# Tile addresses on multiples of 2,048 bytes, paired attention products and normalised probabilities in a two-layer trunk

## Chip, cores and metric

The kernel runs on one core of a Trainium2 chip. The metric is the device time of one execution in microseconds (us). TensorE multiplies a stationary tile, loaded by LDWEIGHTS, with a moving tile that streams past it, and writes PSUM; VectorE (DVE), ScalarE (ACT) and GpSimd (POOL) work on SBUF and PSUM; SyncE (SP) issues most DMAs. The engines run side by side and wait for each other by semaphores.

## What is computed

A trunk of two layers over x of 256 tokens and 1,024 channels, all float32. Cut to what matters:

```python
for l in range(2):
    x = x + 0.5 * swiglu(rms_norm(x, g1), w_gate, w_up, w_down)      # 1024 -> 2816 -> 1024
    z = rms_norm(x, gm) @ w_in[l]                                     # 1024 -> 4 * 512
    q, k, v, p = z split in four                                      # 8 heads of 64
    a = softmax(q @ k.T / 8 + bias, 256 keys, masked) @ v             # per head
    m = pool_scale * (group-linear of (mean over a window of p - p))  # 4 groups of 128
    x = x + concat([a, m]) @ w_out[l]
    x = x + 0.5 * swiglu(rms_norm(x, g2), w_gate2, w_up2, w_down2)
return rms_norm(x, final_norm)
```

## The kernel before, in words

Tokens lie in two tiles of 128 partitions (`t`). Each float32 product of weights is made from three float32r products: weights and activations are split into a high and a low part, and high x high, high x low and low x high are summed (`split_products`, L983, L984 and L986, inside `out_tile`, `down`, `gate_up` and `project_z`; `project_first` has its own copies at L993, L994 and L1043). Every one has a stationary tile of 128 x 128 and moves 512 columns. The weights come by DMA into three slots `w_raw`; ScalarE writes `w_hi` (L467, L474), VectorE writes `w_lo` (L714, L723). The stationary tiles are `xt_hi`/`xt_lo` (normalised activations, transposed; also the input of the output projection) and `gt_hi`/`gt_lo` (gated activations, transposed).

A layer is a feed-forward stage of eleven chunks, a mix stage, and a feed-forward stage. The order on each engine is the order in which its block is written; each engine works through its own list and waits where a semaphore is not there yet.

In the mix stage TensorE's list is `project_z` for the four parts of z (q, k, p, v; eight steps of three matmuls for each token tile), with other work put in behind given steps: transposes of q and k, scores of a head `s(h)` (`head_scores`, L1192, two products of 64 rows, each run as two passes of float32), and transposes of a head's probabilities `t(h)` (L1210). Then follow the pool differences (`pool_differences`, L1235), the pool's linear maps (L1244), probabilities x V (`probs_v`, L1220: the probabilities stationary, 64 columns of V moving), the output projection's first half, the transposes of the heads (L1308) and its second half.

Between them VectorE adds the bias and takes the row maximum (`add_bias`, L830 to L840), ScalarE takes the exponential with its row sum (`exps`, L615), TensorE transposes the unnormalised probabilities, and both engines store the transposed ones over `scores` (`store_probs_t`, L623 and L846). The division by the row sum comes last: one reciprocal for all heads (L900), and two products over the heads' output in PSUM (L915), which is then transposed and split (L669, L923).

SBUF tiles are taken one behind the other in the order of their `sb(...)` lines. Of the sizes in bytes per partition: each w tile 8,192, `resid` and `normed` 8,192, `xt_hi` and `xt_lo` 8,192, `gains` 192, each of three `gain_rows` 512, `final_gain` 4,096, `silu` and `gated` 2,048, `gt_hi` and `gt_lo` 4,096, `bias` 12,288, `mask` 256, `z` 16,384.

Of the kernel before, what the change touches and what calls it, by code (L numbers as in the profile page):

```python
# [24 lines left out]
D_MODEL = 1024  # L25
# [9 lines left out]
N_GROUPS = len(POOL_WINDOWS)  # L35
D_FF = 2816
RMS_EPS = 1e-6

P = 128
# [12 lines left out]
WARM_UP = 8  # L52

# [33 lines left out]
def trunk(nc, x, ffn1_norm, ffn1_w_gate, ffn1_w_up, ffn1_w_down, mix_norm, w_in, rpb, w_pool,  # L87
# [8 lines left out]
    with ctx:  # L96
# [9 lines left out]
        w_lo = [sb(f"w_lo{s}", [P, UNIT], F32R) for s in range(SLOTS)]  # L106
        resid = sb("resid", [P, TT, D_MODEL])
        normed = sb("normed", [P, TT, D_MODEL])
        xt_hi = sb("xt_hi", [P, TT, KT, P], F32R)
        xt_lo = sb("xt_lo", [P, TT, KT, P], F32R)  # L110
        gains = sb("gains", [P, STAGES, DEPTH, KT])
        gain_rows = [sb(f"gain_rows{j}", [DEPTH * KT, P]) for j in range(STAGES)]
        final_gain = sb("final_gain", [P, D_MODEL])
        silu = sb("silu", [P, TT, FC])
        gated = sb("gated", [P, TT, FC])
        gt_hi = sb("gt_hi", [P, 2, 2, TT, P], F32R)
        gt_lo = sb("gt_lo", [P, 2, 2, TT, P], F32R)
        bias = sb("bias", [P, N_HEADS, DELTAS, GRID_W])
        mask = sb("mask", [P, GRID_W])
# [3 lines left out]
        scores = sb("scores", [P, N_HEADS, TT, SEQ])  # L123
        pool_m = sb("pool_m", [P, TT, N_GROUPS, SEQ])
        w_pool_sb = sb("w_pool_sb", [P, N_GROUPS, P])
        pool_scale_sb = sb("pool_scale_sb", [P, N_GROUPS])
        ident = sb("ident", [P, P])
# [4 lines left out]
        zeros = sb("zeros", [P, BANK], F32R)  # L132
# [9 lines left out]
        row_sum = sb("row_sum", [P, TT, N_HEADS])  # L142
        inv_sum = sb("inv_sum", [P, TT, N_HEADS])
# [11 lines left out]

        def heads_out(t):
            return z[:, t, 0, :]
# [56 lines left out]
        heads_stored = sem("heads_stored")  # L214
        heads_t_ready = sem("heads_t_ready")
# [206 lines left out]
        def _(act):  # L422
# [188 lines left out]
            def exps(layer, h):  # L611

                act.wait_ge(max_ready, layer * N_HEADS + (h + 1))
                for t in range(TT):
                    done = nc.scalar.activation(  # L615
                        scores[:, h, t, :], scores[:, h, t, :], ACT.Exp,
                        bias=neg_max[:, h, t:t + 1], accum_out=row_sum[:, t, h:h + 1])
                done.then_inc(probs_ready, 1)
# [7 lines left out]
            def mix_stage(layer):  # L626
# [40 lines left out]
                for t in range(TT):  # L667
                    act.wait_ge(heads_t_ready, layer * 2 + (t + 1))
                    nc.scalar.activation(xt_hi[:, t, 0:4, :], ps[:, 6 + t, :], ACT.Copy  # L669
                                         ).then_inc(heads_t_hi_ready, 1)  # L670
# [31 lines left out]
        def _(dve):  # L702
# [145 lines left out]

            def store_diffs(layer, j):

                dve.wait_ge(diff_ready, layer * 2 + (j + 1))
                nc.vector.tensor_copy(z[:, j, 1, :], ps[:, 4 + j, :]).then_inc(diff_stored, 1)

            def mix_stage(layer):
# [38 lines left out]
                store_probs_t(layer, 5)  # L893
                store_diffs(layer, 0)
# [3 lines left out]

                dve.wait_ge(probs_ready, layer * N_HEADS + N_HEADS)
                nc.vector.reciprocal(inv_sum[:, :, :], row_sum[:, :, :]).then_inc(inv_ready, 1)  # L900
# [11 lines left out]
                dve.wait_ge(inv_ready, layer + 1)  # L912
                dve.wait_ge(pv_ready, layer * N_HEADS + N_HEADS)
                for t in range(TT):
                    nc.vector.tensor_tensor(  # L915
                        heads_out(t).rearrange("p (h d) -> p h d", h=N_HEADS),
                        ps[:, t, :].rearrange("p (h d) -> p h d", h=N_HEADS),
                        inv_sum[:, t, :].rearrange("p (h o) -> p h o", o=1)
                        .to_broadcast([P, N_HEADS, HEAD_DIM]), ALU.mult).then_inc(heads_stored, 1)
                mix_unit(layer, 10)  # L920
                for t in range(TT):
                    dve.wait_ge(heads_t_hi_ready, layer * 2 + (t + 1))
                    nc.vector.tensor_tensor(  # L923
                        xt_lo[:, t, 0:4, :], ps[:, 6 + t, :].rearrange("p (k q) -> p k q", k=4),
                        xt_hi[:, t, 0:4, :].bitcast(F32), ALU.subtract
                    ).then_inc(heads_t_lo_ready, 1)
# [52 lines left out]
        def _(pe):  # L979
# [206 lines left out]
            def head_scores(layer, h):  # L1186
                if h >= 2:

                    pe.wait_ge(biased_ready, layer * N_HEADS + (h - 1))
                rows = slice((h % 2) * HEAD_DIM, (h % 2 + 1) * HEAD_DIM)  # L1190
                for t in range(TT):
                    last = nc.tensor.matmul(ps[:, 4 + h % 2, t * SEQ:(t + 1) * SEQ],  # L1192
                                            q_t[rows, h // 2, t, :], k_t[rows, h // 2, :, :],
                                            start=True, stop=True)
                last.then_inc(scores_ready, 1)
# [19 lines left out]
            def probs_v(layer, h):  # L1215
                wait_probs_t_stored(layer, h)
                for t in range(TT):
                    for k in range(TT):

                        last = nc.tensor.matmul(  # L1220
                            ps[:, t, h * HEAD_DIM:(h + 1) * HEAD_DIM],
                            scores[:, h, k, t * P:(t + 1) * P],
                            z[:, k, 3, h * HEAD_DIM:(h + 1) * HEAD_DIM],
                            start=(k == 0), stop=(k == TT - 1))
                last.then_inc(pv_ready, 1)

            def pool_differences(layer, j):
# [5 lines left out]
                for g in (2 * j, 2 * j + 1):  # L1233
                    for k in range(TT):
                        last = nc.tensor.matmul(  # L1235
                            ps[:, 4 + j, (g % 2) * SEQ:(g % 2 + 1) * SEQ],
                            z[:, k, 2, g * P:(g + 1) * P], pool_m[:, k, g, :],
# [17 lines left out]
            def mix_stage(layer):  # L1255
# [19 lines left out]
                def s(h):  # L1275
                    if h == 0:
                        pe.wait_ge(k_t_stored, layer * 2 + 2)
                    head_scores(layer, h)

                def t(h):  # L1280
# [16 lines left out]
                for h in range(N_HEADS):  # L1297
                    probs_v(layer, h)

                pe.wait_ge(pooled_lo_ready, layer * N_GROUPS + N_GROUPS)  # L1300
                out_tile(layer, 0, 8, 0, True, start=True)
                for k in (1, 2, 3):
                    out_tile(layer, 0, 8 + k // 2, k % 2, True)

                for t in range(TT):
                    pe.wait_ge(heads_stored, layer * 2 + (t + 1))
                    for k in range(4):
                        last = nc.tensor.transpose(ps[:, 6 + t, k * P:(k + 1) * P],  # L1308
                                                   heads_out(t)[:, k * P:(k + 1) * P], ident[:, :])
                    last.then_inc(heads_t_ready, 1)  # L1310
                out_tile(layer, 1, 8, 0, False, start=True)
                out_tile(layer, 1, 8, 1, False).then_inc(w_out_used, 1)
                out_tile(layer, 1, 9, 0, False)
                out_tile(layer, 1, 9, 1, False).then_inc(w_out_used, 1)
                for t in range(TT):
                    pe.wait_ge(heads_t_lo_ready, layer * 2 + (t + 1))
                    for j in (10, 11):
                        for k in range(2):
# [72 lines left out]
```

## Time and profile before

| | us |
|---|---|
| median of 3 runs | 972.66 (971.89 to 972.71) |
| profiled execution | 971.49 |
| its span, first to last instruction | 969.5 |
| TensorE busy | 952.6 (98%) |
| VectorE busy | 548.3 (57%) |
| ScalarE busy | 496.9 (51%) |
| mean granted TensorE clock | 0.997 |

The page gives each engine's busy time, the span in 40 slices, and the costliest groups. Matmuls are pipelined: a row's duration contains the time in which the next one already runs, so the durations add up to more than the span. What a stream of matmuls costs is read from the starts of neighbouring rows. LDWEIGHTS stands under PEld.

### The profile page before, as it was taken

To read this page: it belongs to the slowest core of one execution; us is meant where nothing else is said; L and a number is where in the kernel's file an instruction comes from. 1 tells how busy PE (TensorE), PEld (TensorE's weight loads), DVE (VectorE), ACT (ScalarE), POOL (GpSimd) and SP (SyncE) were. 2 spreads that over 40 slices of the span, in tenths; PEclk is the share of its full clock that TensorE was granted. 3 is DMA by queue.
4 is the path that set the end of the run, shared out by engine and by line. 5 is a ranking of instruction groups with operands and counts; after the bars stand their busy time and mean duration, and the time that the engine had idled before them with its cause. 6 is when DMAs were issued, how large, how long until landed. Compare 5 with 4: busy or idle time off the path is not lost.

```text
span 969.5 us, 12851 instructions
## 1 busy us (share of the span) xinstructions
PE 952.6 (98%) x4379; PEld 777.3 (80%) x4379; DVE 548.3 (57%) x862; ACT 496.9 (51%) x813; POOL 44.7 (5%) x81
## 2 busy tenths in 40 slices
PE   8899999999999999999999999999999999999996
PEld 6688888877788888888888888888778888888885
DVE  5545564557645664655476555455755565455644
ACT  5545454556535554545465455455663365454542
POOL 1010010010001010100010000000100010000000
PEclk9999999999999999999999999999999999999999
DMA  7967868636224978675456657553542266556441
GB/s 242 248 189 175 234 171 281 233 104 242 88 87 136 255 175 227 175 212 186 130 181 214 215 195 250 180 191 124 173 174 88 87 217 212 178 180 209 152 151 44
DMA packets 123532, 174.67 MB, mean 180 GB/s; under 512 B 8384, under 2 KB 99696, under 8 KB 123248
## 3 DMA queue, kind: packets, MB, share of 16 engines
q1 hardware_dynamic: 117744, 165.70, 51.4%
q0 software_dynamic: 2848, 6.38, 5.5%
q10 hardware_dynamic: 2912, 2.22, 0.7%
q8 instruction: 18, 0.29, 0.1%
q14 instruction: 10, 0.08, 0.0%
HBM read 173.14 MB, written 4.19 MB: 183 GB/s over the span
## 4 chain that ended last, share of the span: by engine, by line
PE 93%; DVE 2%; ACT 2%; issue 2%; DMA 1%; SPq 0%; POOL 0%; POOLq 0%; DVEq 0%; ACTq 0%
PE ps L983 28%; PE ps L986 27%; PE ps L984 27%; PE ps L1080 2%; PE ps L1192 2%; PE ps L1220 1%; DVE w_lo L723 1%; PE ps L993 1%; PE ps L994 1%; PE ps L1210 1%; ACT xt_hi L489 1%; PE ps L1235 1%; PE ps L1068 1%; DMA w_raw<-in_ffn_w_down_dram 1%; DVE xt_lo L737 0%
## 5 line engine op out<-in xcount | busy, mean ns | idle before, releaser
L983 PE MATMUL ps<-w_hi,xt_hi 128*128 128x512 f32 x856 | 342.0, 400 | 3.0 <-DVE w_lo L723 1.5
L723 DVE SCALAR_TENSOR_TENSOR w_lo<-w_raw,gains,w_hi 128x512 fp32r<-128x512 f32 x416 | 285.1, 746 | 89.0 <-ACT w_hi L474 87.9
L984 PE MATMUL ps<-w_lo,xt_hi 128*128 128x512 f32 x856 | 333.5, 390 | 0.0
L986 PE MATMUL ps<-w_hi,xt_lo 128*128 128x512 f32 x856 | 329.2, 391 | 0.0
L474 ACT ACTIVATE w_hi<-w_raw,gains 128x512 fp32r<-128x512 f32 x408 | 260.7, 713 | 86.1 <-PE ps L986 81.1
L714 DVE TENSOR_TENSOR w_lo<-w_raw,w_hi 128x1024 fp32r<-128x1024 f32 x104 | 122.7, 1221 | 126.3 <-ACT w_hi L467 126.2
L983 PEld LDWEIGHTS ps<-w_hi,xt_hi 128*128 128x128 f32 x856 | 160.8, 188 | 41.4 <-DVE w_lo L723 4.1
L986 PEld LDWEIGHTS ps<-w_hi,xt_lo 128*128 128x128 f32 x856 | 160.7, 188 | 34.6
L984 PEld LDWEIGHTS ps<-w_lo,xt_hi 128*128 128x128 f32 x856 | 161.0, 188 | 30.3
L467 ACT ACTIVATE w_hi<-w_raw 128x1024 fp32r<-128x1024 f32 x104 | 104.4, 1051 | 114.0 <-PE ps L986 106.6
L983 PE MATMUL ps<-w_hi,gt_hi 128*128 128x512 f32 x352 | 139.0, 395 | 3.6 <-DVE gt_lo L778 3.6
L984 PE MATMUL ps<-w_lo,gt_hi 128*128 128x512 f32 x352 | 138.7, 394 | 0.0
L986 PE MATMUL ps<-w_hi,gt_lo 128*128 128x512 f32 x352 | 110.3, 393 | 0.0
L531 ACT ACTIVATE gt_hi<-ps 128x512 fp32r<-128x512 f32 x40 | 23.9, 597 | 139.8 <-PE ps L1080 139.8
L778 DVE TENSOR_TENSOR gt_lo<-ps,gt_hi 128x512 fp32r<-128x512 f32 x40 | 27.7, 691 | 105.4 <-ACT gt_hi L531 105.4
L983 PEld LDWEIGHTS ps<-w_hi,gt_hi 128*128 128x128 f32 x352 | 66.5, 189 | 18.6 <-DVE gt_lo L778 4.0
L984 PEld LDWEIGHTS ps<-w_lo,gt_hi 128*128 128x128 f32 x352 | 66.6, 189 | 14.1
L986 PEld LDWEIGHTS ps<-w_hi,gt_lo 128*128 128x128 f32 x352 | 66.4, 189 | 14.2
L772 DVE SCALAR_TENSOR_TENSOR gated<-ps,rstd_scaled,silu 128x256 f32<-128x256 f32 x88 | 42.0, 477 | 11.1 <-ACT silu L542 11.1
L542 ACT ACTIVATE silu<-ps,rstd 128x256 f32<-128x256 f32 x88 | 41.5, 472 | 8.8 <-PE ps L986 4.2
L387 POOL DMA_DIRECT2D bias_scratch<-in_rpb_dram x32 | 26.4, 828 | 217.9 <-PE ps L986 209.9
L737 DVE TENSOR_TENSOR xt_lo<-ps,xt_hi 128x512 fp32r<-128x512 f32 x24 | 15.5, 686 | 21.4 <-ACT xt_hi L489 21.4
(87 smaller groups left out, 434.7 us busy)
## 6 DMA issues: line engine op xcount, KB each, us to landing
w_raw<-in_ffn_w_down_dram SPq DMA_DIRECT2D x88, 512.0 KB, 4.3
w_raw<-in_ffn_w_gate_dram SPq DMA_DIRECT2D x86, 512.0 KB, 4.1
w_raw<-in_ffn_w_up_dram SPq DMA_DIRECT2D x86, 512.0 KB, 5.2
w_raw<-in_w_in_dram SPq DMA_DIRECT2D x32, 512.0 KB, 4.9
w_raw<-in_w_out_dram SPq DMA_DIRECT2D x16, 512.0 KB, 5.2
bias_scratch<-in_rpb_dram POOLq DMA_DIRECT2D x32, 96.0 KB, 7.9
bias<-bias_scratch POOLq DMA_DIRECT2D x2, 1536.0 KB, 7.1
pool_m<-in_pool_matrix_dram ACTq DMA_DIRECT2D x1, 1024.0 KB, 8.3
```

What stands on the lines that cost most here:

```text
L387: pool.dma_start(scratch[number, rq * GRID_W:(rq + 1) * GRID_W, i, :] .rearrange("p (d c) -> d p c", d=DELTAS), src).then_inc(bias_rows_lo ...
L467: nc.scalar.activation(w_hi[slot][:, part], w_raw[slot][:, part], ACT.Copy).then_inc(hi_ready[slot], 2)
L474: nc.scalar.activation(w_hi[slot][:, part], w_raw[slot][:, part], ACT.Copy, scale=g).then_inc(hi_ready[slot], 1)
L531: nc.scalar.activation(gt_hi[:, 0, :, :, :], ps[:, 6, :], ACT.Copy).then_inc(gt_hi_ready, 1)
L542: nc.scalar.activation(silu[:, t, :], ps[:, t, 0:FC], ACT.Silu, scale=rstd[:, t, :]).then_inc(silu_ready[t], 1)
L714: nc.vector.tensor_tensor(w_lo[slot][:, part], w_raw[slot][:, part], w_hi[slot][:, part].bitcast(F32), ALU.subtract).then_inc(lo_ready[slo ...
L723: nc.vector.scalar_tensor_tensor(w_lo[slot][:, part], w_raw[slot][:, part], g, w_hi[slot][:, part].bitcast(F32), ALU.mult, ALU.subtract).t ...
L772: nc.vector.scalar_tensor_tensor(gated[:, t, :], ps[:, t, FC:2 * FC], rstd_scaled[:, t, 0:1], silu[:, t, :], ALU.mult, ALU.mult).then_inc( ...
L778: nc.vector.tensor_tensor(gt_lo[:, 0, :, :, :].rearrange("p k t q -> p (k t q)"), ps[:, 6, :], gt_hi[:, 0, :, :, :].rearrange("p k t q -> ...
L983: nc.tensor.matmul(o, hi, wh, start=start, stop=False)
L984: nc.tensor.matmul(o, hi, wl, start=False, stop=False)
L986: last = nc.tensor.matmul(o, lo, wh, start=False, stop=bool(stop))
```

## The change

A pad of 480 words stands in front of all tiles, and the list of tiles is put in another order: first w, xt, gt and zeros, then silu, gated, resid, normed, z, q_t, k_t, scores and the rest whose sizes are multiples of 2,048 bytes, and the small ones last. The scores of two heads are made together (`pair_scores`), the products on rows 0 to 63 and on rows 64 to 127 in turn. Probabilities are normalised on VectorE before they are transposed (`normalise`). V is stationary in `pair_v`, with 64 columns for each head of a pair in its own half of the columns, and moves 256 columns of transposed probabilities; its output is already transposed, so the transposes of the heads and the products with inv_sum go. The second half of the tokens in the pool differences moves only the columns from 120. The order of the mix stage on TensorE and VectorE is written anew.

```diff
+POOL_FROM = 128 - max(POOL_WINDOWS) // 2
+PAGE_PAD = 480
+        sb("page_pad", [P, PAGE_PAD])
         w_raw = ...; w_hi = ...; w_lo = ...
+        xt_hi, xt_lo, gt_hi, gt_lo, zeros, silu, gated
         resid, normed
-        xt_hi, xt_lo, gains, gain_rows, final_gain, silu, gated, gt_hi, gt_lo, bias, mask
         z, q_t, k_t, scores
+        bias, pool_m, final_gain, w_pool_sb, ident, gain_rows, mask, gains
...
+            def normalise(layer, h):
+                dve.wait_ge(probs_ready, layer * N_HEADS + (h + 1))
+                nc.vector.reciprocal(inv_sum[:, h, :], row_sum[:, h, :]).then_inc(inv_ready, 1)
+                dve.wait_ge(inv_ready, layer * N_HEADS + (h + 1))
+                for t in range(TT):
+                    done = nc.vector.tensor_scalar(scores[:, h, t, :], scores[:, h, t, :],
+                                                   inv_sum[:, h, t:t + 1], None, ALU.mult)
+                done.then_inc(normalised_ready, 1)
...
 (VectorE, mix_stage)
                 add_bias(layer, 0)
                 add_bias(layer, 1)
                 mix_unit(layer, 7, halves=(0,))
+                normalise(layer, 0)
+                normalise(layer, 1)
                 add_bias(layer, 2)
+                add_bias(layer, 3)
                 mix_unit(layer, 7, halves=(1,))
-                add_bias(layer, 3)
+                normalise(layer, 2)
+                store_probs_t(layer, 1)
                 add_bias(layer, 4)
-                store_probs_t(layer, 1)
+                normalise(layer, 3)
                 add_bias(layer, 5)
                 mix_unit(layer, 8)
+                normalise(layer, 4)
+                store_probs_t(layer, 3)
+                normalise(layer, 5)
                 add_bias(layer, 6)
-                store_probs_t(layer, 3)
                 add_bias(layer, 7)
                 store_kv(layer, 3, 0)
+                normalise(layer, 6)
                 store_probs_t(layer, 5)
+                normalise(layer, 7)
...
-                for t in range(TT):
-                    nc.vector.tensor_tensor(heads_out(t) ..., ps[:, t, :] ..., inv_sum ..., ALU.mult)
...
+            def pair_scores(layer, pair):
+                if pair >= 1:
+                    pe.wait_ge(biased_ready, layer * N_HEADS + 2 * pair)
+                for t in range(TT):
+                    for e in range(2):
+                        rows = slice(e * HEAD_DIM, (e + 1) * HEAD_DIM)
+                        last = nc.tensor.matmul(ps[:, 4 + e, t * SEQ:(t + 1) * SEQ],
+                                                q_t[rows, pair, t, :], k_t[rows, pair, :, :],
+                                                start=True, stop=True)
+                        if t == TT - 1:
+                            last.then_inc(scores_ready, 1)
...
 (transpose_probs)
-                pe.wait_ge(probs_ready, layer * N_HEADS + (h + 1))
+                pe.wait_ge(normalised_ready, layer * N_HEADS + (h + 1))
...
+            def pair_v(layer, pair):
+                wait_probs_t_stored(layer, 2 * pair)
+                wait_probs_t_stored(layer, 2 * pair + 1)
+                cols = slice((pair % 2) * SEQ, (pair % 2 + 1) * SEQ)
+                for k in range(TT):
+                    for e in range(2):
+                        h = 2 * pair + e
                         last = nc.tensor.matmul(
-                            ps[:, t, h * HEAD_DIM:(h + 1) * HEAD_DIM],
-                            scores[:, h, k, t * P:(t + 1) * P],
+                            ps[e * HEAD_DIM:(e + 1) * HEAD_DIM, pair // 2, cols],
                             z[:, k, 3, h * HEAD_DIM:(h + 1) * HEAD_DIM],
+                            scores[:, h, k, :],
                             start=(k == 0), stop=(k == TT - 1))
...
-                project_z(layer, 2, 1, after={1: lambda: s(1), 3: lambda: s(2),
-                                              5: lambda: (s(3), t(0)), 7: lambda: (s(4), t(1))})
-                project_z(layer, 3, 0, after={1: lambda: (s(5), t(2)), 3: lambda: (s(6), t(3)),
-                                              5: lambda: (s(7), t(4)), 7: lambda: t(5)})
+                project_z(layer, 2, 1, after={3: lambda: s(1), 5: lambda: t(0),
+                                              7: lambda: (s(2), t(1))})
+                project_z(layer, 3, 0, after={1: lambda: t(2), 3: lambda: (s(3), t(3)),
+                                              5: lambda: t(4), 7: lambda: t(5)})
```

## Rows read from the trace of the kernel before

**Rows 1.** The page: busy time of each engine, and the granted clock in 40 slices.
```profile
PE 952.6 (98%) x4379; PEld 777.3 (80%) x4379; DVE 548.3 (57%) x862; ACT 496.9 (51%) x813; POOL 44.7 (5%) x81
PEclk9999999999999999999999999999999999999999
```

**Rows 2.** TensorE's waits: who waited for whom; us in total, times, longest.
```profile
PE ps L983 <- DVE gt_lo L778: 3.6, 1, 3.6
PE ps L983 <- DVE w_lo L723: 1.5, 3, 1.1
PE ps L993 <- ACT xt_hi L489: 1.2, 5, 0.2
```

**Rows 3.** Timeline, gate and up products: start us, duration us, instruction.
```profile
62.06 0.39 PE L983 MATMUL ps<-w_hi,xt_hi 128*128 128x512 f32 x1
...
65.46 0.39 PE L983 MATMUL ps<-w_hi,xt_hi 128*128 128x512 f32 x1
```

**Rows 4.** Timeline, first down product, and what follows the last.
```profile
73.40 0.39 PE L983 MATMUL ps<-w_hi,gt_hi 128*128 128x512 f32 x1
...
78.90 0.39 PE L983 MATMUL ps<-w_hi,xt_hi 128*128 128x512 f32 x1
```

**Rows 5.** Timeline, two products of the output projection.
```profile
289.21 0.39 PE L983 MATMUL ps<-w_hi,xt_hi 128*128 128x512 f32 x1
...
291.93 0.39 PE L983 MATMUL ps<-w_hi,xt_hi 128*128 128x512 f32 x1
```

**Rows 6.** Timeline behind the longest wait, with the halved clock.
```profile
38.64 0.63 PE L984 MATMUL ps<-w_lo,gt_hi 128*128 128x512 f32 x1
39.07 0.63 PE L983 MATMUL ps<-w_hi,gt_hi 128*128 128x512 f32 x1
39.50 0.63 PE L984 MATMUL ps<-w_lo,gt_hi 128*128 128x512 f32 x1
```

**Rows 7.** Chain of work, mix stage of layer 0: start us, us, what.
```profile
261.99 1.73 PE ps L1235 x8
...
270.40 7.09 PE ps L1220 x64
...
283.04 0.87 PE ps L1308 x8
```

**Rows 8.** Windows: all engines; L983 alone; L993 alone (us, busy, PEclk, DMA).
```profile
38.60:39.50 0.90, 0.90 (x4) 0.67 (x3) 0.90 (x2) 0.90 (x3) 0.00 (x0) 0.50 1.15 135
...
40.00:969.50 929.50, 466.47 (x1174) 1.00 0.57 178
...
40.00:969.50 929.50, 16.18 (x40) 1.00 0.57 178
```

**Rows 9.** Timeline around one head's scores.
```profile
234.82 0.40 PE L986 MATMUL ps<-w_hi,xt_lo 128*128 128x512 f32 x1
235.15 1.13 PE L1192 MATMUL ps<-k_t,q_t 64*128 64x256 f32 x4
236.20 0.50 PE L983 MATMUL ps<-w_hi,xt_hi 128*128 128x512 f32 x1
236.54 0.39 PE L984 MATMUL ps<-w_lo,xt_hi 128*128 128x512 f32 x1
```

**Rows 10.** VectorE's groups: instruction, count, busy us, mean ns, idle before.
```profile
L974 DVE TENSOR_SCALAR normed<-z,rstd 128x512 f32<-128x512 f32 x1 | 0.5, 488 | 0.7 <-POOL rstd L417 0.7
L900 DVE RECIPROCAL inv_sum<-row_sum 128x16 f32<-128x16 f32 x2 | 0.5, 242 | 0.0
```

**Rows 11.** Timeline of VectorE and ScalarE around mix unit 8.
```profile
247.30 0.42 DVE L833 CUSTOM_DVE_ANT_0 scores<-ps,bias 128x256 f32<-128x256 f32 x1 [1.05 <-issue]
248.11 0.17 DVE L840 TENSOR_SCALAR neg_max<-row_max 128x2 f32<-128x2 f32 x1
248.18 0.68 DVE L846 COPY scores<-ps 128x512 f32<-128x512 f32 x1
251.40 0.50 ACT L615 ACTIVATE scores<-scores,neg_max 128x256 f32<-128x256 f32 x1
252.39 2.00 ACT L467 ACTIVATE w_hi<-w_raw 128x1024 fp32r<-128x1024 f32 x2
253.53 2.36 DVE L714 TENSOR_TENSOR w_lo<-w_raw,w_hi 128x1024 fp32r<-128x1024 f32 x2 [2.23 <-ACT w_hi L467]
```

More of the change, by code:

```diff
@@ L106, in trunk @@
         w_lo = [sb(f"w_lo{s}", [P, UNIT], F32R) for s in range(SLOTS)]
+        xt_hi = sb("xt_hi", [P, TT, KT, P], F32R)
+        xt_lo = sb("xt_lo", [P, TT, KT, P], F32R)
+        gt_hi = sb("gt_hi", [P, 2, 2, TT, P], F32R)
+        gt_lo = sb("gt_lo", [P, 2, 2, TT, P], F32R)
+        zeros = sb("zeros", [P, BANK], F32R)
+        silu = sb("silu", [P, TT, FC])
+        gated = sb("gated", [P, TT, FC])
         resid = sb("resid", [P, TT, D_MODEL])
         normed = sb("normed", [P, TT, D_MODEL])
[L109 to L119, printed above, removed]
         z = sb("z", [P, TT, 4, 512])
@@ L123, in trunk @@
         scores = sb("scores", [P, N_HEADS, TT, SEQ])
+        bias = sb("bias", [P, N_HEADS, DELTAS, GRID_W])
         pool_m = sb("pool_m", [P, TT, N_GROUPS, SEQ])
+        final_gain = sb("final_gain", [P, D_MODEL])
         w_pool_sb = sb("w_pool_sb", [P, N_GROUPS, P])
+        ident = sb("ident", [P, P])
+        gain_rows = [sb(f"gain_rows{j}", [DEPTH * KT, P]) for j in range(STAGES)]
+        mask = sb("mask", [P, GRID_W])
+        gains = sb("gains", [P, STAGES, DEPTH, KT])
         pool_scale_sb = sb("pool_scale_sb", [P, N_GROUPS])
-        ident = sb("ident", [P, P])
         wait_mark = sb("wait_mark", [P, 1])
@@ L666, in mix_stage @@
                 mix_unit(layer, 10)
-                for t in range(TT):
-                    act.wait_ge(heads_t_ready, layer * 2 + (t + 1))
-                    nc.scalar.activation(xt_hi[:, t, 0:4, :], ps[:, 6 + t, :], ACT.Copy
-                                         ).then_inc(heads_t_hi_ready, 1)
+                for b in range(2):
+                    act.wait_ge(pv_ready, layer * 4 + (2 * b + 2))
+                    nc.scalar.activation(
+                        xt_hi[:, :, 2 * b:2 * b + 2, :],
+                        ps[:, b, :].rearrange("p (g t q) -> p t g q", g=2, t=TT), ACT.Copy
+                    ).then_inc(heads_t_hi_ready, 1)
                 mix_unit(layer, 11)
@@ L897, in mix_stage @@
                 store_probs_t(layer, 7)
-                dve.wait_ge(probs_ready, layer * N_HEADS + N_HEADS)
-                nc.vector.reciprocal(inv_sum[:, :, :], row_sum[:, :, :]).then_inc(inv_ready, 1)
                 store_kv(layer, 3, 1)
@@ L911, in mix_stage @@
                         ALU.mult, ALU.subtract).then_inc(pooled_lo_ready, 1)
-                dve.wait_ge(inv_ready, layer + 1)
-                dve.wait_ge(pv_ready, layer * N_HEADS + N_HEADS)
-                for t in range(TT):
+                mix_unit(layer, 10)
+                for b in range(2):
+                    dve.wait_ge(heads_t_hi_ready, layer * 2 + (b + 1))
                     nc.vector.tensor_tensor(
[L916 to L925, printed above, removed]
+                        xt_lo[:, :, 2 * b:2 * b + 2, :],
+                        ps[:, b, :].rearrange("p (g t q) -> p t g q", g=2, t=TT),
+                        xt_hi[:, :, 2 * b:2 * b + 2, :].bitcast(F32), ALU.subtract
                     ).then_inc(heads_t_lo_ready, 1)
@@ L1184, in transpose_heads @@
                 last.then_inc(qk_t_ready, 1)
[L1186 to L1190, printed above, removed]
+            def pair_scores(layer, pair):
+                if pair >= 1:
+                    pe.wait_ge(biased_ready, layer * N_HEADS + 2 * pair)
                 for t in range(TT):
[L1192 to L1195, printed above, removed]
+                    for e in range(2):
[5 more added lines that the diff above has]
+                            last.then_inc(scores_ready, 1)
             def wait_probs_t_stored(layer, h):
@@ L1234, in pool_differences @@
                     for k in range(TT):
+                        first = POOL_FROM * k
                         last = nc.tensor.matmul(
-                            ps[:, 4 + j, (g % 2) * SEQ:(g % 2 + 1) * SEQ],
-                            z[:, k, 2, g * P:(g + 1) * P], pool_m[:, k, g, :],
+                            ps[:, 4 + j, (g % 2) * SEQ + first:(g % 2 + 1) * SEQ],
+                            z[:, k, 2, g * P:(g + 1) * P], pool_m[:, k, g, first:],
                             start=(k == 0), stop=(k == TT - 1))
@@ L1273, in heads_k, with s @@
                     transpose_heads(layer, 1, h)
-                def s(h):
-                    if h == 0:
+                def s(pair):
+                    if pair == 0:
                         pe.wait_ge(k_t_stored, layer * 2 + 2)
-                    head_scores(layer, h)
+                    pair_scores(layer, pair)
                 def t(h):
@@ L1296, in mix_stage @@
                 pe.wait_ge(z_kv_stored, layer * 4 + 4)
-                for h in range(N_HEADS):
-                    probs_v(layer, h)
+                for pair in range(N_HEADS // 2):
+                    pair_v(layer, pair)
                 pe.wait_ge(pooled_lo_ready, layer * N_GROUPS + N_GROUPS)
-                out_tile(layer, 0, 8, 0, True, start=True)
-                for k in (1, 2, 3):
-                    out_tile(layer, 0, 8 + k // 2, k % 2, True)
                 for t in range(TT):
[L1306 to L1314, printed above, removed]
+                    out_tile(layer, t, 8, 0, t == 0, start=True)
+                    last = out_tile(layer, t, 8, 1, t == 0)
+                    if t == 1:
+                        last.then_inc(w_out_used, 1)
+                    out_tile(layer, t, 9, 0, t == 0)
+                    last = out_tile(layer, t, 9, 1, t == 0)
+                    if t == 1:
+                        last.then_inc(w_out_used, 1)
                 for t in range(TT):
-                    pe.wait_ge(heads_t_lo_ready, layer * 2 + (t + 1))
                     for j in (10, 11):
+                        if t == 0:
+                            pe.wait_ge(heads_t_lo_ready, layer * 2 + (j - 9))
                         for k in range(2):
```

16 lines of the change are left out of this document (4 added, 12 removed).

## The prediction

> **What bounds the kernel now.** I read the page first: TensorE is busy 98% of the span, and its granted clock is full in all 40 slices [rows 1]. The waits of TensorE come next: the longest is 3.6 us, once, near the start, and all the others together are about 5 us [rows 2]. So nothing but TensorE's own stream sets the time from 40 us on, and what a matmul costs is the distance between the starts of two neighbours, not its duration. That distance is the third view, the timeline of single instructions. In the gate and up products 15 matmuls lie between 62.06 and 65.46 us: 226.7 ns each [rows 3]. In the down products 24 lie between 73.40 and 78.90 us: 229.2 ns each [rows 4]. In the output projection 12 lie between 289.21 and 291.93 us: 226.7 ns again [rows 5]. All have 512 columns of float32r, and there are 3,744 of them (856, 352 and 40 times three forms).
>
> The same instruction at the halved clock starts every 0.43 us [rows 6], with 0.50 as its clock [rows 8], and 512 columns at 1.2 GHz are 427 ns. Two array clocks per column of a float32 pass with 256 columns are also 512 clocks, and eight such passes take 1.73 us, 216 ns each [rows 7]. At full clock 512 clocks are 213.3 ns. So the float32r matmul, which reads its 2,048 bytes per partition at full rate, pays 11 to 13 ns that neither the half-rate pass nor the slow clock shows. The rest of the argument turns on what these 11 to 13 ns are.
>
> **Part 1: the addresses.** The pad of 480 words is 1,920 bytes, and if it brings the first tile to a multiple of 2,048, the tiles began at byte 128. By the sizes in the list, each 512-column slice of w_hi and w_lo then starts at 128 beyond such a multiple and crosses one boundary; xt_hi and xt_lo start at 128, and gt_hi and gt_lo, behind gains and gain_rows, at 1,856. After the change all start at 0 and no slice of w crosses. Two things bear on whether this matters. The output projection and the down products run the same helper with the same kind of w slices and the same order of PSUM banks. They differ in the stationary tile, xt against gt, and their pitches differ by 2.5 ns [rows 4, 5]. So an address, by all the rows show, does reach the pitch. And the slices of pool_m, at 64 beyond a multiple, cross a boundary in every second group, and all passes take 216 ns [rows 7]; a crossing that costs is thus one that the full read rate exposes, as is anything else that costs at full rate. The rows don't tell a crossing from a fixed cost of each float32r matmul. I take the crossing, because the pitch moved with an address in the one place where the rows allow a comparison.
>
> The pitch after is bounded by 213.3 and 226.7 ns (no change), and below a gain by the worse phase, 229.2 ns everywhere. I take 215.5, the float32 pass, which has the same count of array clocks. After 40 us there are 1,174 + 40 matmuls of each form [rows 8], some 3,640, of which 1,056 read gt. The sum is 2,584 x 11.2 ns = 28.9 us and 1,056 x 13.7 ns = 14.5 us: 43.4 us. What lies before 40 us is left out, since the first weights are still arriving: TensorE waits there for gt_lo [rows 2], whatever its pitch.
>
> Against this stands the Trainium skill, TensorE: Matmul & The Clock Gate, part 2, on loading the stationary operand: the engine has two independent SBUF read ports, and loading the next weights takes nothing from the running matmul. By that reading an address pair has no say, the 2.5 ns between xt and gt would be unexplained, and part 1 would bring nothing; it is rival A. The same page gives 215.7 ns for 512 columns of bf16 at full clock, which as an estimate would make the sum 42.6 us.
>
> **Part 2: score pairs in row halves.** Today each head is a visit of four passes with 64 rows. From the last projection matmul before to the second behind, 234.82 to 236.54 us, it takes 1.72 us [rows 9]; without a change of the array's shape this would be two distances of 0.227 and four of 0.216, 1.32 us. A visit thus costs 0.40 us of emptying and bare weight loads. Eight visits become four: 1.6 us per layer. Within a pair, two passes on one row half now alternate with two on the other. No row shows two halves at once. Bounds: nothing overlaps (0), or at each of the three changes of half one pass hides (3 x 0.216 x 4 pairs = 2.6 us). I take 2.6, since the halves share neither rows nor a PSUM bank.
>
> **Part 3: V stationary in column halves.** Today 64 passes with 64 columns take 7.09 us [rows 7], 111 ns each, the pace of the weight loads, as the transposes' 109 ns is. Then 32 passes of 256 columns come: serial 32 x 0.216 + 0.40 for a new shape = 7.3 us; with the halves side by side 17 x 0.216 + 0.40 = 4.1 us. The gain is between -0.2 and 3.0 us; I take 3.0, for the same reason as above. The Trainium skill's TensorEngine Tiling, key properties, says both things, that a change of mode drains the engine and that tiles run in parallel; the first agrees with the 0.40 us, the second no run here shows yet.
>
> **Part 4: small ones.** The head transposes go: 0.87 us per layer [rows 7]. The pool differences of the second token half shrink from 256 to 136 columns: 8 passes x (216 - 115) = 0.8 us. Fewer VectorE operations stand behind the heads, but nobody waited for them: four output tiles (5.4 us) lay between. The copy to xt_hi and xt_lo now has eight tiles (11 us) of cover for about 3 us of work. Without that cover it would cost those 3 us. The reordered tiles of other engines cost nothing that any row prices. No DMA and no queue order on SyncE or GpSimd is touched.
>
> **Part 5: what is added, normalise.** On VectorE, per head, a reciprocal (under 0.24 us) and two products of 256 columns. The nearest row is an SBUF to SBUF product of 512 columns at 0.49 us [rows 10]; I take 0.7 us per head until TensorE may go, bounds 0.5 and 1.0. Eight are 5.6 us per layer, on an engine busy 57% [rows 1]; the load is no matter, the order is. Transposes of head h now wait for normalise(h), and behind that wait the whole projection stream is queued. The worst place is t(4): normalise(4) stands behind mix_unit(8), which waits for ScalarE. From the end of the third score pair the chain is: transposes of head 1 and the signal 0.9, copy 0.6, add_bias(4) 0.9, normalise(3) 0.55, add_bias(5) 1.0, the exponentials 1.0, ScalarE's first half of unit 8 1.0, VectorE's two halves 2.3, normalise(4) 0.7 [rows 10, 11]: 9.0 us. TensorE has before t(4) three sets of four transposes (1.6), six steps of three matmuls (4.0) and a score pair (1.4): 7.0 us. It waits 2.0 us. By the same bookkeeping t(0) waits 0.4 us behind unit 7, the third pair 0.2 for its banks, t(6) 0.5: about 3.1 us per layer, and 0.4 more when the projection steps are shorter. Bounds: 1 and 5 us.
>
> **Sum.** Parts 2 to 4 give 1.6 + 2.6 + 3.0 + 0.9 + 0.8 = 8.9 us per layer, less 3.5 us of waits: 5.4, for two layers 10.8 us. With part 1: 54.2 us. The profiled execution took 971.5 us, with a span of 969.5; it would become 917.3. The median stands 1.2 us above it, so 918.5.
>
> **Rivals.** A: the 11 ns belong to every float32r matmul and stay. For it: there is no warm row of the same matmul at another w address. Against it: 226.7 against 229.2. Waits are then 3.1: 972.7 - 2 x 5.8 = 961; if only gt's 2.5 ns go (1,056 x 2.5 = 2.6 us), 958.5.
> B: the pitch falls, but the halves don't run side by side. Scores lose 2.6 and PV 3.2 us per layer, while t(4)'s wait shrinks by some 0.6: 918.5 + 2 x 5.2 = 929.
> C: part of the pitch goes (half): about 940.
> D: neither pays: 961 + 10.4 = 971.5, within 0.2%.
> E, slower: with every tile on a multiple of 2,048 stationary and moving reads always start in the same phase and collide. Its place is each float32r matmul, its price 3.7 us per ns of pitch. With the mix stage's gain of 11.6 it turns the sign from +3.1 ns; at +4 ns the time is 976. For it speaks only that the pitch does move with an address; against it, that xt and w start in the same phase today and are the faster pair.
>
> **How the numbers follow.** Forecast 0.42, A 0.33, B 0.12, C 0.06, D 0.04, E 0.03. The forecast's own range is 911 (pitch 213.4) to 927. For 8 in 10 the range must hold A as well, so it runs from 912 to 964; D, E and the ends of others are left out. A measurement of this kernel tells 0.2%, 2 us, from no change. Faster: all but D, E and a sliver, 0.93; same 0.04; slower 0.03.
>
> **What would show it.** The distance of two gate and up matmuls: 215.5 (forecast) or 226.7 (A). The down products should have the same distance, since their tile gets the same phase. A score pair of eight passes: 1.3 us side by side or 1.9 in a row. PV: 3.7 or 6.9 us. In the waits of TensorE new lines should stand, for VectorE's scores, some 6 us, the longest near 2 us at t(4). A pitch of 216 with a time above 935 would mean that another engine or the weights' DMA has become the bound in the feed-forward stages; busy shares of VectorE and ScalarE under 65% say no.

## The result, and the profile after

| | before | changed |
|---|---|---|
| median, us | 972.31 (971.89 to 972.71) | 960.17 (958.90 to 960.97) |
| ratio | | 0.9874, 95% interval 0.9857 to 0.9891 |
| profiled execution, us | 971.49 | 958.90 |
| its span, us | 969.5 | 957.0 |

The change makes the kernel 1.3% faster, 12.1 us. The forecast was 918.5 us, and the range from 912 to 964 held the time only because it reached to rival A, which had 961 or, with the 2.5 ns of gt, 958.5.

The page of the changed kernel, TensorE's busy time and the granted clock in 40 slices, as in [rows 1]:

```profile
PE 932.1 (97%) x4299; PEld 760.1 (79%) x4299; DVE 555.6 (58%) x904; ACT 496.2 (52%) x813; POOL 44.6 (5%) x81
PEclk9999999999999999999999999999999999999999
```

The timeline of the changed kernel gives the distances (start us, duration us, instruction). Between the first two rows lie 21 gate and up matmuls, between the third and the fourth 24 down products:

```profile
61.68 0.39 PE L992 MATMUL ps<-w_hi,xt_hi 128*128 128x512 f32 x1
...
66.44 0.39 PE L992 MATMUL ps<-w_hi,xt_hi 128*128 128x512 f32 x1
...
73.03 0.39 PE L992 MATMUL ps<-w_hi,gt_hi 128*128 128x512 f32 x1
...
78.47 0.39 PE L992 MATMUL ps<-w_hi,xt_hi 128*128 128x512 f32 x1
```

The gate and up products kept their 226.7 ns (4.76 us / 21), against [rows 3]. The down products went from 229.2 ns in [rows 4] to 226.7 (5.44 / 24). So by the sizes of the tiles no slice of w crosses a boundary any more, and the 11 ns are still there; only the 2.5 ns between xt and gt have gone. (No row shows an address: that the pad brings the first tile to a multiple of 2,048 bytes is taken from its size.)

The start of each stage shows where the 12.5 us of span came from. These are the first transposes of the residual in the mix stage, the second feed-forward stage, and the next layer's first; before, then changed:

```profile
202.85 0.82 PE L1068 MATMUL ps<-ident,resid 128*128 128x128 f32 x6
300.10 0.60 PE L1068 MATMUL ps<-ident,resid 128*128 128x128 f32 x4
488.27 0.93 PE L1068 MATMUL ps<-ident,resid 128*128 128x128 f32 x7
```

```profile
202.07 0.60 PE L1077 MATMUL ps<-ident,resid 128*128 128x128 f32 x4
294.08 0.92 PE L1077 MATMUL ps<-ident,resid 128*128 128x128 f32 x7
481.74 1.03 PE L1077 MATMUL ps<-ident,resid 128*128 128x128 f32 x8
```

The mix stage fell from 97.25 to 92.01 us, the feed-forward stage behind it from 188.17 to 187.66. In layer 1 the mix stage is 4.9 us shorter. Two mix stages make 10.1 us, the four feed-forward stages 2.0 and the start before the first 0.4.

In the mix stage a pair's scores now take what one head's took (1.72 us in [rows 9]): 1.74 us, from the last matmul before to the second behind. V's 32 passes end after 3.6 us, where 64 took 7.09 [rows 7]:

```profile
233.96 0.40 PE L995 MATMUL ps<-w_hi,xt_lo 128*128 128x512 f32 x1
234.29 1.13 PE L1202 MATMUL ps<-k_t,q_t 64*128 64x256 f32 x8
235.35 0.50 PE L992 MATMUL ps<-w_hi,xt_hi 128*128 128x512 f32 x1
235.70 0.40 PE L993 MATMUL ps<-w_lo,xt_hi 128*128 128x512 f32 x1
...
268.54 3.67 PE L1234 MATMUL ps<-scores,z 128*64 128x256 f32 x32
272.14 0.50 PE L992 MATMUL ps<-w_hi,xt_hi 128*128 128x512 f32 x1
```

Eight passes need four distances, 32 need sixteen: two always start together, 6 or 7 ns apart. And the waits of TensorE, which had no such lines in [rows 2] (us in total, times, longest):

```profile
PE ps L1221 <- DVE scores L856: 7.0, 6, 2.4
PE ps L992 <- DVE gt_lo L779: 3.6, 1, 3.6
...
PE ps L1202 <- DVE row_max L834: 1.0, 4, 0.3
```

The longest is the one of head 4:

```profile
254.49 0.66 PE L1221 MATMUL ps<-ident,scores 128*128 128x128 f32 x4 [2.36 <-DVE scores L856]
```

### The profile page after: what moved, and what is told of

Same layout as the page of the kernel before. It is cut to its first block and busy times, and to the rows that moved or that the text cites. A ratio compares the mean times of both kernels' runs of the same rounds, so it can differ in the third digit from the quotient of the medians.

```text
span 957.0 us, 12739 instructions
## 1 busy us (share of the span) xinstructions
PE 932.1 (97%) x4299; PEld 760.1 (79%) x4299; DVE 555.6 (58%) x904; ACT 496.2 (52%) x813; POOL 44.6 (5%) x81
## 5 line engine op out<-in xcount | busy, mean ns | idle before, releaser
L993 PE MATMUL ps<-w_lo,xt_hi 128*128 128x512 f32 x856 | 334.2, 390 | 0.0
L993 PEld LDWEIGHTS ps<-w_lo,xt_hi 128*128 128x128 f32 x856 | 161.4, 189 | 30.8
L993 PE MATMUL ps<-w_lo,gt_hi 128*128 128x512 f32 x352 | 137.7, 391 | 0.0
L993 PEld LDWEIGHTS ps<-w_lo,gt_hi 128*128 128x128 f32 x352 | 66.4, 189 | 13.6
```

The lines of the kernel that those rows point to most:

```text
L993: nc.tensor.matmul(o, hi, wl, start=False, stop=False)
```

## The experiments

Three questions: whether the addresses alone make the 2.5 ns, and by what rule; what the 11 ns are; and what stands behind the new waits.

### Addresses alone, and all the rest alone

The kernel before with the new list of tiles and the pad, nothing else:

```diff
+        sb("page_pad", [P, PAGE_PAD])
         w_raw, w_hi, w_lo
+        xt_hi, xt_lo, gt_hi, gt_lo, zeros, silu, gated, resid, normed, ...
```

> The kernel before with nothing but the pad and the new order of the tiles (part 1 alone). Theory S (the pitch follows the phase of the stationary tile against the moving one, and only gt was out of phase): the distance of the down products falls from 229.2 to 226.7 ns, that of gate and up products stays at 226.7; 1,056 x 2.5 ns = 2.6 us, so 969.7. Theory N (the addresses do nothing alone, and gt's pitch fell for another reason of the change): 972.3. The theory of the prediction (crossings cost 11 ns) would want 929.

Measured: 969.98 us, ratio 0.9971 (0.9960 to 0.9982) to the kernel before, 972.91 beside it: 2.9 us. The down products stand 226.9 ns apart in the mean, where 229.1 stood; those with xt do not change.

The changed kernel with the old list:

```diff
-        sb("page_pad", [P, PAGE_PAD])
+        (the list of the kernel before)
```

> The changed kernel with the old list of tiles and no pad (parts 2 to 5 alone). Theory S: down products at 229.2 ns again, 960.2 + 2.6 = 962.8. Theory N: 960.2, and the down products at 226.7. The mix stages should stay as in the changed kernel, 92.0 and 92.4 us.

Measured: 962.86 us, ratio 0.9904 (0.9892 to 0.9917). The distance of the down products is back; between these rows lie 24:

```profile
74.32 0.39 PE L991 MATMUL ps<-w_hi,gt_hi 128*128 128x512 f32 x1
...
79.81 0.39 PE L991 MATMUL ps<-w_hi,xt_hi 128*128 128x512 f32 x1
```

5.49 / 24 = 228.8 ns. Both came out within 0.3 us of theory S. The two parts add up: 2.9 us for the addresses and 10.0 for the rest, against 12.1 for the whole, of which each is known to about 1 us.

### What the 11 ns are

Rows of float32r matmuls on two tiles of ones, in place of the warm-up. The kernel ran once; what is read from it is the distances inside a row. A part of them:

```diff
-            for n in range(WARM_UP):
-                last = nc.tensor.matmul(ps[:, n % 2, :], zeros[:, 0:P], zeros[:, :], ...)
+            for n in range(13):
+                last = nc.tensor.matmul(ps[0:128, n % 2, 0:512], st[:, 0:128], mv[:, 256:768], ...)
+            for n in range(13):
+                last = nc.tensor.matmul(ps[0:128, n % 2, 0:256], st[:, 0:128], mv[:, 0:256], ...)
+            for n in range(13):
+                last = nc.tensor.matmul(ps[0:64, n % 2, 0:512], st[:, 0:64], mv[:, 0:512], ...)
```

> The changed kernel with rows of 13 float32r matmuls in place of the warm-up, all with the same two tiles of ones: moving and stationary start moved by 64, 128 and 1,024 bytes, 256 and 384 in place of 512 columns, 64 and 32 stationary columns, and a bf16 row. Its time is no measure of the change (some 40 us more). Theory F (11 to 13 ns are a fixed cost of each float32r matmul): 512, 384 and 256 columns cost 226.7, 173.3 and 120 ns, fewer stationary columns change nothing, bf16 216. Theory L (the weight load takes read slots from the moving stream): with 64 and 32 stationary columns the distance falls by half and three quarters of 13 ns, to 220 and 217. Theory C (a boundary crossed, the prediction's): moving starts moved by 64 and 128 bytes cost 11 ns more than the aligned ones. Theory S: a start moved by 64 bytes on one side alone gives 229.2, moved by 128 or on both sides 226.7.

The timeline of the probe, a row for each 13 matmuls: the moving start moved by 1,024 bytes (so that 512 columns cross a boundary), the stationary start moved by 64 bytes, then, further down, 256 columns, 384 columns, 64 and 32 stationary columns, and bf16:

```profile
23.36 3.16 PE L1356 MATMUL ps<-xt_hi,xt_lo 128*128 128x512 f32 x13
26.35 3.19 PE L1358 MATMUL ps<-xt_hi,xt_lo 128*128 128x512 f32 x13
...
38.40 1.72 PE L1366 MATMUL ps<-xt_hi,xt_lo 128*128 128x256 f32 x13
39.95 2.42 PE L1368 MATMUL ps<-xt_hi,xt_lo 128*128 128x384 f32 x13
42.20 3.15 PE L1370 MATMUL ps<-xt_hi,xt_lo 128*64 128x512 f32 x13
45.19 3.17 PE L1372 MATMUL ps<-xt_hi,xt_lo 128*32 128x512 f32 x13
48.20 2.98 PE L1374 MATMUL ps<-xt_hi,xt_lo 128*128 128x512 bf16 x13
```

After most changes of operands up to nine distances of a row with 512 columns are unsettled (224 to 238 ns), so a row's mean can be 4 ns above its settled value. Settled, from the last distances of a row, are: with the crossing 226.7, as without; 384 columns 173.3; 256 columns 120; bf16 216. Taken from these, 512, 384 and 256 columns at 2.4 GHz are 213.3, 160.0 and 106.7 ns, and each time 13.3 are left. So the rest is fixed for each float32r matmul and has nothing to do with the columns read: theory F. Theory C falls, since a crossed boundary costs nothing. Theory L falls too: with 64 and 32 stationary columns the distance does not shrink, it even grows, to 230 and 231.5; why is open. That the bf16 row has 2.6 ns in place of 13.3 says that this is a property of float32r, not of 512 columns. Why float32r has it is open.

Of the Trainium skill, TensorE: Matmul & The Clock Gate, part 1: N / 2.4 + 2.5 ns from start to start, for a matmul with N moving columns on the warm array. It holds for the bf16 row (216, it gives 215.7), not for float32r, where the last term is 13.3. The float32 passes of 256 columns stand 215.4 ns apart, which fits it only if each of their columns counts as two.

### The rule of the phase

Four rows of the first probe already differed with the starts, and not as theory S had it there. It wanted 229.2 ns for 64 bytes on either side and 226.7 for 128. The stationary start moved by 64 bytes gave 233.3, the moving one 228.9, and 128 bytes on either side 232.4; only 64 bytes on both sides came out as expected, 226.7. A second probe, also run once, moved the starts against each other:

> The changed kernel with rows of 20 float32r matmuls in place of the warm-up, stationary and moving starts moved against each other by 32 to 512 bytes. If the distance follows the difference of the two starts modulo 128 bytes, moves by 256 and 512 bytes cost nothing and those by 192 and 384 cost as 64 and 0. If modulo 256: 256 and 512 cost nothing, 192 on the stationary side costs what 64 on the moving side costs (229). If modulo 512: 256 costs something too.

Rows of 20, from its timeline. The stationary start was moved by 192, 256, 384, 512 and 64 bytes, in this order, then (next but one) the moving one by 192:

```profile
17.62 4.74 PE L1352 MATMUL ps<-xt_hi,xt_lo 128*128 128x512 f32 x20
22.20 4.72 PE L1354 MATMUL ps<-xt_hi,xt_lo 128*128 128x512 f32 x20
26.76 4.81 PE L1356 MATMUL ps<-xt_hi,xt_lo 128*128 128x512 f32 x20
31.41 4.70 PE L1358 MATMUL ps<-xt_hi,xt_lo 128*128 128x512 f32 x20
35.94 4.83 PE L1360 MATMUL ps<-xt_hi,xt_lo 128*128 128x512 f32 x20
...
45.27 4.83 PE L1364 MATMUL ps<-xt_hi,xt_lo 128*128 128x512 f32 x20
```

| stationary minus moving start, bytes | settled distance, ns |
|---|---|
| 0, 256, 512, -256, -512 | 226.7 |
| 192, -64 | 228.9 |
| 128, -128, 384 | 232.4 |
| -384 | 233.3 |
| 32, 64, -192 | 233.3 |

The difference counts modulo 256 bytes: 192 and -64 agree, 64 and -192 agree, 256 and 512 are as good as 0. Only -384 is 1 ns off the others of its class, which is open. In the kernel before gt starts at 1,856 and w at 128; 1,728 modulo 256 is 192, and its 229.2 ns are within 0.3 of the second line of the table. Even the single distances agree: both there and in the probe's row they go 226, 229, 232, 225, 230, 231. xt had a difference of 0. That is all that the addresses of part 1 were worth.

To see the rule in the kernel, 16 words between w and the rest:

```diff
+        sb("phase_pad", [P, 16])
         xt_hi = sb("xt_hi", [P, TT, KT, P], F32R)
```

> The changed kernel with 16 words between the w tiles and all tiles behind them, so that xt and gt start 64 bytes behind a multiple of 2,048 and w on one. Theory S with the distances of the probe (stationary start moved by 64 bytes: 233.5 ns, against 226.7): all float32r matmuls with both stationary tiles cost 6.8 ns more; some 3,640 of them after the start make 25 us: 985. The rival: in a kernel whose moving tile changes with each matmul the phase counts less than in the probe, the 2.5 ns of gt everywhere: 9 us, 969.

Measured, in two executions: 980.13 us, ratio 1.0086 (1.0066 to 1.0106) to 971.83 beside it: 20 us over the changed kernel, slower than the kernel before. The distance is the probe's; 21 matmuls lie between these rows, 4.90 / 21 = 233.3 ns:

```profile
62.81 0.39 PE L993 MATMUL ps<-w_hi,xt_hi 128*128 128x512 f32 x1
...
67.71 0.40 PE L993 MATMUL ps<-w_hi,xt_hi 128*128 128x512 f32 x1
```

The sum of 25 us was 5 too high. Part of that is that the distances behind transposes were never at 226.7 (in each chunk some six, of 228 to 236 ns), so they lose less; a feed-forward stage became 4.6 us longer (192.2, from 300.53 to 492.76 us, against 187.7), where 792 x 6.7 ns is 5.3.

And the changed kernel without its pad, so that all tiles start 128 bytes behind a multiple of 2,048:

```diff
-        sb("page_pad", [P, PAGE_PAD])
```

> The changed kernel without the pad, its list of tiles as it is: every tile that TensorE reads starts 128 bytes behind a multiple of 2,048, stationary and moving alike, and each 512-column slice crosses a boundary. Theory S (only the difference of the two starts modulo 256 bytes counts): nothing changes, 226.7 ns for all products and 960. The rival (the multiples of 2,048 are worth something by themselves): a distance over 227 ns, each ns of it 3.7 us.

Measured: 959.87 us, ratio 0.9888 (0.9869 to 0.9908). The distances are those of the changed kernel, 226.9 ns for the down products in the mean. The pad does nothing, and neither do the multiples of 2,048. A last probe, run once:

> The changed kernel with rows of 20 float32r matmuls in place of the warm-up. Both starts moved by 16, 32 and 128 bytes: if the difference alone counts, 226.7 for all; the probe before gave 228 to 232 for 16 bytes, so a start must also be a multiple of some 32 or 64 bytes. Then 64-row halves in turn: two float32r matmuls of 512 columns on the two row halves. If the fixed 13 ns belong to one stream of matmuls, the pair takes 226.7 ns together; if the two halves cover each other's 13 ns, 214 to 216. Last a row that stays in one PSUM bank: 226.7 if the bank has no say.

```profile
17.81 4.76 PE L1352 MATMUL ps<-xt_hi,xt_lo 128*128 128x512 f32 x20
22.41 4.74 PE L1354 MATMUL ps<-xt_hi,xt_lo 128*128 128x512 f32 x20
...
36.20 4.85 PE L1361 MATMUL ps<-xt_hi,xt_lo 64*128 64x512 f32 x40
40.98 4.85 PE L1363 MATMUL ps<-xt_hi,xt_lo 128*128 128x512 f32 x20
```

Both starts at 16 bytes gave 230 ns (first row, 229 and 231 in turn), both at 32 or 128 bytes 226.7. So an equal difference is not enough: 16 bytes behind a tile's start is a bad place for both, 32 bytes are a good one, and others than 16, 32, 64 and 128 were not run. The 40 matmuls on row halves start two by two, 3 to 4 ns apart, and a pair takes 226.7 once settled: the halves run side by side, but they don't cover each other's 13 ns. One PSUM bank instead of two makes no difference.

### The waits for normalised scores

First only the longest one:

```diff
                 add_bias(layer, 5)
-                mix_unit(layer, 8)
                 normalise(layer, 4)
                 store_probs_t(layer, 3)
+                mix_unit(layer, 8)
                 normalise(layer, 5)
```

> The changed kernel with normalise(4) and store_probs_t(3) ahead of mix_unit(8) in VectorE's list. If the longest wait (2.4 us in each layer, transposes of head 4) comes from VectorE standing at unit 8 while the exponentials of head 4 are long done, it goes, and 2 x 2.0 to 2.4 us come back: 955.4 to 956.2. The rival: what is late next is unit 8's low part or add_bias(6), which move back with it or stay where they were, and less than 1 us is won in all: over 959.

Measured: 957.04 us, ratio 0.9840 (0.9827 to 0.9853), between the two theories: 3.1 us won, not 4 to 5. The waits for normalised scores fell from 7.0 to 4.4 us, the longest from 2.4 to 1.1. Head 4 no longer waits; late next are heads 5 and 6, whose steps still stand behind unit 8.

```profile
PE ps L1221 <- DVE scores L856: 4.4, 6, 1.1
```

```profile
257.77 0.66 PE L1221 MATMUL ps<-ident,scores 128*128 128x128 f32 x4 [0.56 <-DVE scores L856]
260.94 0.66 PE L1221 MATMUL ps<-ident,scores 128*128 128x128 f32 x4 [1.12 <-DVE scores L856]
```

Then all of VectorE's list by when its input comes:

```diff
                 add_bias(layer, 1)
+                normalise(layer, 0)
+                normalise(layer, 1)
                 mix_unit(layer, 7, halves=(0,))
-                normalise(layer, 0)
-                normalise(layer, 1)
...
                 add_bias(layer, 5)
-                mix_unit(layer, 8)
                 normalise(layer, 4)
-                store_probs_t(layer, 3)
                 normalise(layer, 5)
                 add_bias(layer, 6)
+                store_probs_t(layer, 3)
                 add_bias(layer, 7)
-                store_kv(layer, 3, 0)
                 normalise(layer, 6)
+                mix_unit(layer, 8)
+                store_kv(layer, 3, 0)
```

> The changed kernel with VectorE's list in the order in which the scores and exponentials come: normalise(0) and (1) ahead of unit 7, normalise(4), (5), add_bias(6), (7) and normalise(6) ahead of unit 8. If the waits of TensorE for normalised scores and free banks (7.0 + 1.0 us) are all due to the place of the weight units, they go: 960.2 - 8 = 952.2, or 4.8 under the kernel with normalise(4) moved alone. The rival: the exponentials of ScalarE, queued behind its part of unit 8, are late next and leave 2 us or more of the waits: 954 or above.

Measured: 949.65 us, ratio 0.9776 (0.9763 to 0.9790), 10.5 us under the changed kernel, where 8 were expected, and the fastest of all. (The two were measured beside different runs of the kernel before; by the ratios it is 9.5 us.) None of the waits of the mix stage is left:

```profile
PE ps L992 <- DVE gt_lo L779: 3.3, 1, 3.3
PE ps L1343 <- DVE zeros L704: 1.5, 1, 1.5
PE ps L1002 <- ACT xt_hi L488: 1.2, 5, 0.2
```

Its mix stage runs from 202.18 to 289.42 us:

```profile
202.18 1.03 PE L1077 MATMUL ps<-ident,resid 128*128 128x128 f32 x8
289.42 0.82 PE L1077 MATMUL ps<-ident,resid 128*128 128x128 f32 x6
```

87.2 us against 92.0: 4.8 us for 4.0 us of listed waits. In layer 1 it is 87.2 against 92.4, 5.1 us, but there a wait for w_lo, 0.5 us in its row, is gone too. A wait costs more than its row. At t(4) of the changed kernel the last matmul before and the first transpose are 2.76 us apart, where the reordered kernel has 0.23, so the place costs 2.53 for the 2.36 of the row; and the four transposes then take 0.41 us in place of 0.35:

```profile
251.73 0.40 PE L995 MATMUL ps<-w_hi,xt_lo 128*128 128x512 f32 x1
254.49 0.66 PE L1221 MATMUL ps<-ident,scores 128*128 128x128 f32 x4 [2.36 <-DVE scores L856]
254.90 0.47 PE L992 MATMUL ps<-w_hi,xt_hi 128*128 128x512 f32 x1
```

### Halves not in turn

```diff
-                for t in range(TT):
-                    for e in range(2):
+                for e in range(2):
+                    for t in range(TT):
                         rows = slice(e * HEAD_DIM, (e + 1) * HEAD_DIM)
```

and the same in `pair_v`.

> The changed kernel with the same products, but both of one half before both of the other half, in the scores and in the products with V. In the changed kernel the passes start two by two, 7 ns apart, every 216 ns: 4 distances for a pair's scores, 16 for the products with V. Theory T (only neighbours in the list run side by side): a pair's eight passes take 7 distances (one overlap where the half changes), V's 32 passes 24 or 25; per layer 4 x 3 + 8 or 9 distances more, 4.4 us, for two layers up to 8.8 us, less what the waits for normalised scores take up: 965 to 969. The rival (the engine looks further ahead and pairs them anyway): 960.

Measured: 959.00 us, ratio 0.9870 (0.9855 to 0.9885): theory T falls. The eight passes of a pair still take no longer than in turn:

```profile
234.32 0.40 PE L995 MATMUL ps<-w_hi,xt_lo 128*128 128x512 f32 x1
234.65 1.14 PE L1202 MATMUL ps<-k_t,q_t 64*128 64x256 f32 x8
235.72 0.50 PE L992 MATMUL ps<-w_hi,xt_hi 128*128 128x512 f32 x1
236.05 0.39 PE L993 MATMUL ps<-w_lo,xt_hi 128*128 128x512 f32 x1
```

1.73 us, with two passes starting 13 ns apart in place of 7. With V the two are 13 and then 57 to 59 ns apart, and still there is one such pair every 216 ns. So the two halves need not alternate in the list: here four passes of one half stand before four of the other. The trace does not name the halves of a pair, and what looks ahead, and how far, these runs don't show.

## Why the prediction was wrong

**What bounds the kernel** was read rightly: TensorE's stream, and in it the distance between starts.

**Part 1 failed**, and in one sentence: "I take the crossing, because the pitch moved with an address in the one place where the rows allow a comparison." The two facts were separate. The 2.5 ns between xt and gt do come from an address, from the difference of two starts modulo 256 bytes, and they went as theory S says (2.9 us measured, 2.6 by the sum). The 11 to 13 ns are a fixed 13.3 ns of each float32r matmul, which rows at another width would have shown, and the trace of before has none. So 40.5 of the 43.4 us never existed. An effect of 2.5 ns was used as evidence for one of 11, and the sentence before it in the prediction had said that the rows can't tell the two apart; the chance of 0.42 against 0.33 did not follow from rows, and the likeliest case should have been the one in which only the 2.5 ns that the rows show go: 958.5, which is 1.7 from the median.

The sentence of the Trainium skill, TensorE: Matmul & The Clock Gate, part 2, on two independent read ports agrees with the probe as far as the 11 ns go: with 32 stationary columns in place of 128 the moving stream gains nothing. But the phase between the two starts costs up to 6.7 ns, so an address pair does have a say, which that sentence does not lead one to expect; where the two reads meet is open.

**Parts 2 and 3** were right in kind and too low. For the scores the prediction let three of eight passes hide, and four do; for V it had 15 of 32 hidden and 0.40 us for the new shape, where 16 are and the whole takes 3.60 us. Scores: 4 x 1.74 in place of 8 x 1.72 us, less the two matmuls' share of 0.454 in each visit: 10.1 to 5.1, a gain of 5.0 (4.2 forecast). V: 7.09 to 3.60, a gain of 3.5 (3.0). For V the outcome was partly luck: the reason given was that the halves share neither rows nor a PSUM bank, but the two column halves of `pair_v` use all rows and write the same bank.

**Part 4** was right: the sum of all gains, read from the reordered kernel that has no waits, is 97.25 - 87.24 = 10.0 us per layer, of which scores and V make 8.5, which leaves 1.5 for the transposes and the pool differences (1.7 forecast). The pool differences by themselves gave the 0.8 forecast: two rows of eight passes take 1.49 us each, where they took 1.89.

**Part 5** was right in place and mechanism. The waits came at t(4), t(0), t(6) and the third pair, 2.4, 0.5, 0.6 and 0.3 us in layer 0, where 2.0, 0.4, 0.5 and 0.2 stood (and 0.4 more in all with shorter steps); the fourth pair also waited 0.2 us, which the prediction did not have. In sum the list has 4.0 us per layer, and their cost is 4.8, where 3.1 to 3.5 was forecast. Normalise itself took 0.72 us for a head from its reciprocal to the next operation on VectorE, as taken.

So the mix stages gave 10.1 us where 10.8 were forecast, and that nearness is luck in part: per layer the errors in gross gain (+1.1) and in waits (+1.3) nearly cancel. **Rivals:** A held, with gt's 2.5 ns gone. B and D fell with the halves side by side, C with gate and up products that kept their 226.7 ns. E fell, and its mechanism is the wrong way round: it let equal starts collide, but equal starts are the ones that cost nothing, and unequal ones cost. Its price, 3.7 us per ns, was somewhat high: 64 bytes more between w and xt add 6.7 ns and 20 us, enough to turn the sign.

## What to carry to other kernels

Where TensorE's stream is the bound, compare the distances of matmuls that differ in one thing only, and claim of a gap no more than that comparison shows; for the rest, a row of some twenty matmuls (the first nine distances can be unsettled) at two or three widths tells a fixed cost from one per column in one run. Keep stationary and moving starts of float32r matmuls equal modulo 256 bytes, and on multiples of 32 as far as these runs tell. When work is put on an engine whose list also holds weight splits, place each step by when its input arrives, ahead of splits that nobody needs soon: here that won back about 10 us, all that the new order had lost to waits in the mix stages.

## What was not expected of the hardware

- A float32r matmul costs its columns at 2.4 GHz plus 13.3 ns: 120, 173.3 and 226.7 ns for 256, 384 and 512 columns; a bf16 matmul of 512 columns costs its columns plus 2.6 ns, a float32 pass of 256 columns two clocks a column plus 2.1 ns (215.4).
- The difference of the stationary and the moving start, modulo 256 bytes, adds 0 (at 0), 2.2 (192), 5.7 to 6.7 (128) or 6.7 ns (32, 64) to a float32r matmul of 512 columns. Crossing a multiple of 2,048 adds none.
- Two float32 passes on different row or column halves run side by side, one pair every 216 ns, in turn (6 to 7 ns apart) or not (13 to 59); a float32r pair on row halves takes 226.7 ns together.
